# First mixing layer: small products and value products spread over all 24 hops of a round, gate weights in another load, key products later

## What is computed

```python
xr, xw, xk, xv, xa, xg = (h + xx * mu[j] for j in range(6))
r, k, v = xr @ wr, xk @ wk, xv @ wv
a = sigmoid(a0 + (xa @ a1) @ a2)
g = sigmoid(xg @ g1) @ g2
kk = k * k_k normalised per head;  k = k * (1 + (a - 1) * k_a)
# per head of 64: S_t = S_{t-1} diag(w_t) + (S_{t-1} a_t) b_t^T + v_t k_t^T ; y_t = S_t r_t
y = (y - mean) * rsqrt(var + eps) * ln_w + ln_b   # per head
y = (y + sum(r * k * r_k) * v) * g
out = y @ wo
```

## Time and profile before

| | us |
|---|---|
| median of 3 runs | 3449.25 (3448.60 to 3453.86) |
| the profiled execution, device time | 3456.56 |
| its span, first to last instruction | 3454.8 |
| PE / DVE / ACT / POOL busy in the span | 3274.0 / 1647.8 / 754.1 / 362.6 |
| mean granted TensorE clock | 0.974 |

### The profile page before, as it was taken

The page is one execution under the profiler, slowest core; times in us unless marked ns, Lnnn a source line. Parts: engine busy times, 40 slices in busy tenths (PEclk is TensorE's granted clock), DMA queues, the critical chain, the costliest instruction groups (busy, mean ns, idle before and its releaser), DMA issues.

```text
span 3454.8 us, 45620 instructions
## 1 busy us (share of the span) xinstructions
PE 3274.0 (95%) x19462; PEld 2055.7 (60%) x19462; DVE 1647.8 (48%) x3209; ACT 754.1 (22%) x1572; POOL 362.6 (10%) x282
## 2 busy tenths in 40 slices
PE   7999988999999999999999899998999999899998
PEld 3455556888884746788886444544445546434343
DVE  4565675779652226778732666664212304201011
ACT  2333332210013025211002333232223310211111
POOL 0111110222010000132000111113000001000000
PEclk9999998999999999999999999998999999899999
DMA  6322203356641320256522111000211114699997
GB/s 201 122 74 64 69 7 111 110 171 195 194 136 38 98 61 1 61 179 188 170 75 74 49 38 37 26 25 1 70 55 43 49 52 145 284 421 421 421 421 281
DMA packets 355771, 452.46 MB, mean 131 GB/s; under 512 B 25712, under 2 KB 282992, under 8 KB 331760
## 3 DMA queue, kind: packets, MB, share of 16 engines
q1 hardware_dynamic: 355568, 449.55, 38.0%
HBM read 445.27 MB, written 4.20 MB: 130 GB/s over the span
## 4 chain that ended last, share of the span: by engine, by line
PE 83%; DVE 8%; ACT 4%; DMA 3%; issue 1%; SPq 0%; POOLq 0%; POOL 0%; DVEq 0%; ACTq 0%
PE bank L79 82%; DVE A L70 2%; ACT A L87 2%; DMA A<-in_w_up 2%; DVE A L76 1%; DVE A L73 1%; ACT A L86 1%; PE bank L82 1%; DMA W<-in_w_up 1%; DVE A L2023 1%; ACT SM L87 1%; DVE H L70 0%; DVE X L76 0%; DVE X L70 0%; DMA A<-in_x 0%
## 5 line engine op out<-in xcount | busy, mean ns | idle before, releaser
L79 PE MATMUL bank<-A 64*64 64x64 f32 (+6 forms) x8800 | 908.8, 287 | 65.5 <-ACT A L87 37.3
L79 PEld LDWEIGHTS bank<-A 64*64 64x64 f32 (+3 forms) x8800 | 686.1, 157 | 358.3 <-issue 107.7
L79 PE MATMUL bank<-A,W 128*128 128x256 f32 (+1 forms) x2240 | 724.9, 478 | 8.4 <-DMA W<-in_rw_g 7.1
L79 PE MATMUL bank<-H,W 128*128 128x512 f32 (+2 forms) x1712 | 657.2, 528 | 34.1 <-ACT H L87 14.4
L79 PEld LDWEIGHTS bank<-A,W 128*128 128x128 f32 x2240 | 419.9, 191 | 262.4 <-issue 215.3
L87 ACT ACTIVATE A<-bank 128x512 f32<-128x512 f32 (+4 forms) x469 | 194.0, 418 | 1322.0 <-PE bank L79 1225.9
L79 PEld LDWEIGHTS bank<-H,W 128*128 128x128 f32 (+1 forms) x1712 | 309.3, 191 | 275.6 <-issue 238.3
L79 PE MATMUL bank<-A,H 128*64 128x512 f32 (+2 forms) x1224 | 310.7, 574 | 5.4 <-DMA A<-in_w_up 2.6
L70 DVE TENSOR_TENSOR A<-bank,A 128x256 f32<-128x256 f32 (+1 forms) x350 | 157.9, 462 | 195.5 <-PE bank L79 174.7
L87 ACT ACTIVATE A<-A 128x512 f32<-128x512 f32 (+1 forms) x238 | 137.9, 610 | 393.3 <-DVE A L70 362.7
L70 POOL TENSOR_TENSOR A<-A 128x512 f32<-128x512 f32 (+1 forms) x103 | 146.1, 1425 | 709.1 <-PE bank L82 358.7
(11 more groups left out here) (189 smaller groups left out, 2575.4 us busy)
## 6 DMA issues: line engine op xcount, KB each, us to landing
A<-in_w_gate SPq DMA_DIRECT2D x47, 1024.0 KB, 22.7
W<-in_mod_w SPq DMA_DIRECT2D x45, 1024.0 KB, 7.0
A<-in_w_up SPq DMA_DIRECT2D x42, 1024.0 KB, 19.3
A<-in_w_down SPq DMA_DIRECT2D x35, 1024.0 KB, 27.0
W<-in_mlp_up SPq DMA_DIRECT2D x64, 512.0 KB, 5.4
W<-in_mlp_down SPq DMA_DIRECT2D x128, 256.0 KB, 4.0
W<-in_w_mod SPq DMA_DIRECT2D x24, 1024.0 KB, 5.3
W<-in_w_up SPq DMA_DIRECT2D x22, 1024.0 KB, 19.3
```

The costliest lines, as they stand in the source:

```text
L79: return self.e.matmul(o, l, r, start=start, stop=stop, skip_group_check=True)
```

## The change

- PE's fetch products go by a table: four matmuls in hops 2, 5, 8, 11, two in 14, one in 15, three in 17, one each in 22 and 23 (before: four in 14 and four in 17). The v product so ends in hop 23; its ACT copy moves there from hop 18. The small product `row0` of rounds 1 and 2 moves from hop 20 to 17.
- PE's sb halves go to hops 0 and 1 (both in 0 before), sk to 3 and 6 (2 and 4), the variance to 9 (7), bon to 20 (17). The turn of V uses bank 3 instead of 2.
- DVE's masks move with them, and its kh, bh, rkk go to hops 15, 16, 17 (13, 14, 15); the two last post products to hop 16 (14). The transpose of the first mask is now in hop 2, behind the first md step of hop 1.
- POOL's b goes from hop 10 to 14, behind ett; the products "end" to hops 6 and 7 (5 and 6).
- The gate weights of blocks 0 to 3 come with the rv load of blocks 4 to 7, in its free half; the separate rg loads stay for blocks 4 to 7, in rounds 8 to 11.

```diff
+        def gate_parts(ct, off):
+            cs = slice(ct * 128, ct * 128 + 128)
+            return (off, (0, P), (128,), a["rw_g2"][0:128, cs]), (off + 128, (0, 32), (128,), a["rw_g2"][128:160, cs])
...
+        FILL = {2: 4, 5: 4, 8: 4, 11: 4, 14: 2, 15: 1, 17: 3, 22: 1, 23: 1}
+
         def sp_fetch(sp, ct):
             cs = slice(ct * 128, ct * 128 + 128)
             load(sp, ("rk", ct), (0, (0, P), (8, 128), rows128(a["rw_wk"][:, cs])), (1024, (0, P), (8, 128), rows128(a["rw_wr"][:, cs])))
-            load(sp, ("rv", ct), (0, (0, P), (8, 128), rows128(a["rw_wv"][:, cs])))
+            load(sp, ("rv", ct), (0, (0, P), (8, 128), rows128(a["rw_wv"][:, cs])), *(gate_parts(ct - 4, 1024) if ct >= 4 else ()))
...
-            yield from idle(2)
-            for j, name in enumerate(("k", "r", "v")):
-                key = ("rv", ct) if j == 2 else ("rk", ct)
-                s_, there = ring[key]
...
-                b = fbank(ct, j)
-                pe.wait_ge(ring.sems[s_], there)
-                pe.wait_ge(*left[b])
-                for k in range(KT):
+            n = 0
+            for slot in range(24):
+                for n in range(n, n + FILL.get(slot, 0)):
+                    j, k = divmod(n, KT)
+                    name, key = ("k", "r", "v")[j], ("rv", ct) if j == 2 else ("rk", ct)
...
+                    b = fbank(ct, j)
+                    if k == 0:
+                        pe.wait_ge(ring.sems[s_], there)
+                        pe.wait_ge(*left[b])
                     pe.wait_ge(s_dv, ndv["xm", (1, 0, 2)[j], k])
                     m = pe.mm(BK[b][:, :], v[:, k, :], xm[(1, 0, 2)[j]][:, k, :], k == 0, k == 7)
                     if k == 7:
@@ -844,22 +852,21 @@
                             npe.mark_next("free", *key)
                         m.then_inc(s_pe, npe(name, ct))
                         left[b] = (s_ac, nac[name, ct])
...
-                    if k % 4 == 3:
-                        yield from idle(3)
-            if ct in (1, 2):
-                pe_row0(pe, ct - 1)
-            yield from idle(4)
+                n += 1 if slot in FILL else 0
+                if slot == 17 and ct in (1, 2):
+                    pe_row0(pe, ct - 1)
+                yield
...
             for j, (name, dst) in enumerate((("k", Kb2), ("r", Rb2), ("v", V2))):
-                yield from idle(6)
+                yield from idle((6, 6, 11)[j])
...
-            yield from idle(6)
+            yield
...
-            yield from idle(13)
+            yield from idle(16)
             pe.wait_ge(s_dv, ndv["rkk", ct])
             pe.wait_ge(*left[3])
             pe.mm(BK[3][:, :], C("blk"), t0, True, True).then_inc(s_pe, npe("bon", ct))
             left[3] = (s_dv, ndv["bo", ct])
-            yield from idle(7)
...
         def gp_prep(gp, ct):
-            yield from idle(10)
+            yield from idle(14)
             if ct:
                 gp.wait_ge(s_pe, npe["tok", ct - 1, 2])
             gp.wait_ge(s_dv, ndv["kkn", ct])
             gp.wait_ge(s_ac, nac["ab", ct])
             gp.tt(BH, KKb, Ab, MUL).then_inc(s_gp, ngp("b", ct))
-            yield from idle(14)
...
-            yield
+            yield from idle(3)
...
@@ -996,7 +1003,7 @@
             yield
             dv.wait_ge(s_dv, ndv["rh", ct])
             dv.stt(t0, Rb, col("rw_rk", ct), Kb, MUL, MUL).then_inc(s_dv, ndv("rkk", ct))
-            yield from idle(6)
+            yield from idle(4)
...
             score(BH, 4, 0).then_inc(s_pe, npe("sb", ct, 0))
+            yield
             score(BH, 5, 1).then_inc(s_pe, npe("sb", ct, 1))
             yield
...
             pe.wait_ge(*left[2])
             score(KH, 2, 0).then_inc(s_pe, npe("sk", ct, 0))
             left[2] = (s_dv, ndv["sk", ct, 0])
-            yield
-            yield
+            yield from idle(3)
             pe.wait_ge(*left[2])
             score(KH, 2, 1).then_inc(s_pe, npe("sk", ct, 1))
             left[2] = (s_dv, ndv["sk", ct, 1])
-            yield
-            for n, (src, b) in enumerate(((V, 2), (c8(KH), 2), (c8(BH), 3))):
-                yield
-                yield
+            for n, (src, b) in enumerate(((V, 3), (c8(KH), 2), (c8(BH), 3))):
+                yield
+                if n:
+                    yield
                 pe.wait_ge(*((s_gp, ngp["end", ct, n - 1]) if n else (s_ac, nac["v", ct])))
                 pe.wait_ge(*left[b])
                 turn(src, b).then_inc(s_pe, npe("tok", ct, n))
...
-            yield from idle(3)
+            yield from idle(4)
             gp.wait_ge(s_pe, npe["sk", ct, 1])
             gp.wait_ge(s_ac, nac["f", ct])
             for n, src in enumerate((KH, BH)):
                 gp.tt(c8(src), c8(src), per_chunk(Fs[ct % 3]), MUL).then_inc(s_gp, ngp("end", ct, n))
                 yield
-            yield from idle(7)
+            yield from idle(6)
...
-            for n, (dst, b) in enumerate(((Vts[ct % 2], 2), (KHts[ct % 2], 2), (BHts[ct % 2], 3))):
+            for n, (dst, b) in enumerate(((Vts[ct % 2], 3), (KHts[ct % 2], 2), (BHts[ct % 2], 3))):
...
             masked("sb", NRs[ct % 2], 4, 0)
+            yield
             masked("sb", NRs[ct % 2], 5, 1)
             dv.wait_ge(s_dv, ndv.n)
             dv.e.transpose(of16(AM), by16(NRs[ct % 2][:, :, 0, :])).then_inc(s_dv, ndv("raw", ct))
-            yield
...
             for j in range(1, 15):
                 if j not in (1, 8, 12):
                     yield
-                if j == 2:
+                if j == 3:
                     masked("sk", AKs[ct % 2], 2, 0)
-                if j == 4:
+                if j == 6:
                     masked("sk", AKs[ct % 2], 2, 1)
                 solve16(dv, XI, XTMP, j).then_inc(s_dv, ndv() if j < 14 else ndv("inv", ct))
...
         def sp_post(sp, ct):
-            cs = slice(ct * 128, ct * 128 + 128)
-            load(sp, ("rg", ct), (0, (0, P), (128,), a["rw_g2"][0:128, cs]), (128, (0, 32), (128,), a["rw_g2"][128:160, cs]))
+            load(sp, ("rg", ct), *gate_parts(ct, 0))
...
         def pe_post(pe, ct, left):
-            kg, tg = ring["rg", ct]
+            kg, tg = ring["rv", ct + 4] if ct < 4 else ring["rg", ct]
+            off = 1024 if ct < 4 else 0
...
             left[3] = (s_dv, ndv["yc", ct])
-            yield from idle(5)
+            yield from idle(7)
             pe.wait_ge(s_ac, nac["ysq", ct])
             pe.wait_ge(*left[3])
             pe.mm(BK[3][:, :], C("blk"), t2, True, True).then_inc(s_pe, npe("yvar", ct))
             left[3] = (s_dv, ndv["yv", ct])
-            yield from idle(5)
+            yield from idle(3)
             pe.wait_ge(ring.sems[kg], tg)
             pe.wait_ge(s_ac, nac["lo", 4])
             pe.wait_ge(*left[2])
-            pe.mm(BK[2][:, :], wv(kg, 0, (0, P), (128,)), ZG[:, 0:512], True, False)
-            npe.mark_next("free", "rg", ct)
-            pe.mm(BK[2][:, :], wv(kg, 128, (0, 32), (128,)), ZG[0:32, 512:1024], False, True).then_inc(s_pe, npe("g", ct))
+            pe.mm(BK[2][:, :], wv(kg, off, (0, P), (128,)), ZG[:, 0:512], True, False)
+            if ct >= 4:
+                npe.mark_next("free", "rg", ct)
+            pe.mm(BK[2][:, :], wv(kg, off + 128, (0, 32), (128,)), ZG[0:32, 512:1024], False, True).then_inc(s_pe, npe("g", ct))
...
-            yield from idle(6)
+            yield from idle(7)
...
-            yield from idle(12)
+            yield from idle(11)
...
-            yield from idle(5)
...
-            yield from idle(5)
+            yield from idle(6)
             dv.wait_ge(s_pe, npe["yvar", ct])
             dv.ts(t2, BK[3][:, :], 1.0 / 64, 64e-5, MUL, ADD).then_inc(s_dv, ndv("yv", ct))
             yield from idle(3)
...
-            yield from idle(3)
+            yield from idle(4)
             dv.wait_ge(s_ac, nac["yl", ct])
             dv.tt(Yb, Yb, yg[:, ct, :], ADD).then_inc(s_dv, ndv())
             dv.wait_ge(s_dv, ndv.n)
...
             dv.tt(yg[:, ct, :], Yb, BK[2][:, :], MUL).then_inc(s_dv, ndv("post", ct))
-            yield from idle(10)
...
                 if r < 8:
                     sp_fetch(sp, r)
                     sp_mod0(sp, r)
-                if r >= 4:
+                if r >= 8:
                     sp_post(sp, r - 4)
```

More of the change, by code:

```diff
@@ L826, in sp_fetch @@
             load(sp, ("rk", ct), (0, (0, P), (8, 128), rows128(a["rw_wk"][:, cs])), (1024, (0, P), (8, 128), rows128(a["rw_wr"][:, cs])))
-            load(sp, ("rv", ct), (0, (0, P), (8, 128), rows128(a["rw_wv"][:, cs])))
+            load(sp, ("rv", ct), (0, (0, P), (8, 128), rows128(a["rw_wv"][:, cs])), *(gate_parts(ct - 4, 1024) if ct >= 4 else ()))
         def pe_fetch(pe, ct, left):
-            yield from idle(2)
-            for j, name in enumerate(("k", "r", "v")):
-                key = ("rv", ct) if j == 2 else ("rk", ct)
-                s_, there = ring[key]
-                v = wv(s_, 1024 * (j % 2), (0, P), (8, 128))
-                b = fbank(ct, j)
-                pe.wait_ge(ring.sems[s_], there)
```

(14 more changed lines are left out.)

## The result

The changed kernel takes 3470.89 us (median of 6 runs, 3461.49 to 3472.28) where the kernel before takes 3453.58 (6 runs, 3448.60 to 3458.30): a ratio of 1.0046, interval 1.0034 to 1.0058. It is slower by some 16 us, where 27 us less were forecast. The profiled execution took 3471.7 us with a span of 3469.9, against 3456.56 and 3454.8.

What follows compares the result with a forecast made beforehand. PE was taken as the bound, 83% of the chain. Rounds 4 to 7 gave 20.6 us, round 3 1.3, round 8 2, rounds 1, 2 and 9 3: 27 less, 3422 us; range 3408 to 3440 at 0.8.

Steps and rivals of the forecast that it cites:

- the fillings: Work put into hops 1, 3, 6, 9, 15 and 22 hides PE's waits: 6 x 0.49 = 2.9 us a round.
- the solver: Hop 16: with key products moved behind DVE's transposes, PE's wait of 0.95 us at the solver level goes.
- DVE hides it all: Rival: md lands at 6 us or ACT's queue isn't in the way, no 2.0 stall; 41 us gained, 3408; chance 0.13.
- The gate step: Hop 12: gate weights landing with rv remove a wait of 1.78 us and 0.17 of drain, 1.95 us a round.
- One filling of the six: Hop 22: one product matmul put there was to hide 0.49 us a round.
- the md step: Start of round: the later md load makes PE wait in hops 3, 6 and 8; 2.0 us, low 0, high 4.8.
- Two gate issues add 0.8: SP's queue behind rv: two issues of about 0.4 us each, so md lands at 7.6 us into the round.
- The hop by hop working: PE's waits behind md: 0 to 0.2 in hop 3, 0.5 in hop 6, 1.1 for the uu copy; 1.8 to 2.1 together.
- slower: Rival: md lands at 10.1 us or more, rounds 3 to 7 wait 4.8 and PE's clock falls, 2.3 more; 3457; chance 0.07.
- the signs that the prediction named for its failure: DVE waits in hops 16 to 18, mod_w wait past 9 us, clocks under 1.00 in rounds 2 to 7, round 7 above 55.
- Rounds 0, 10, 11: 0, the order of PE's work hardly changes.: First round and last two: no gain or loss counted, 0 us.
- rv is now marked free in hop 23 and not 17: SP's in-order queue: a round's first md load can't be issued before the round begins; named as the edit that costs.

Runs made afterwards that it cites:

- the best kernel: The changed kernel with the ring's turn moved on by four and md loaded ahead of rv on SP: 3417.38 us, ratio 0.9887 to the kernel before.
- the run with the mean later: The changed kernel with the mean four hops later, yc and the squares three: 3463.99 us, ratio 1.0026 to the kernel before.
- the turn: The changed kernel with the ring's turn moved on by four after the rg loads: 3459.32 us, ratio 1.0009 to the kernel before; also added to other runs.
- md first: The changed kernel with SP's order rk, md, md, rv in place of rk, rv, md, md: 3425.31 us, ratio 0.9915 to the kernel before.
- step later: The changed kernel with every md step of DVE one hop later, load as late as there: 3431.01 us, ratio 0.9926 to the kernel before.
- gates alone: The kernel before with only the gate weights of blocks 0 to 3 moved into rv's loads: 3444.02 us, ratio 0.9960.

## Why the prediction was wrong

**Right: what the fillings, the gates and the solver are worth.** 6.0 us a round at the upper clock and 8.3 with a fall were summed; 5.7 and 7.9 to 8.1 were measured once md was out of the way. The rival "DVE hides it all" was priced at 41 us; the best kernel gained 38.5 (3455.92 to 3417.38). The gate step alone was 1.95 and measured 2.0. One filling of the six is not borne out: with hop 22 empty the rounds are as short (50.6), where 0.49 us were summed for it.

**Wrong: the md step, in three places.** It was put at 2.0 us a round (low 0, high 4.8) and took 7.3 to 8.7, with the clock fall in it (58.0 to 59.4 less 50.7). (1) *When it lands.* "Two gate issues add 0.8" gave 7.6 us. SP needed 1.05 to 2.54 us for them, and DVE got md 8.5 to 9.8 us into the round; from rv's issue 8.5 to 9.6, where without gates it was 6.64 and 7.0 and 7.3 in rounds 2 and 3 of the changed kernel. I had counted the parts' issue only, at the least that one takes. The longer issue is not all of it: with the longest, 2.54 us in round 6, md came soonest (8.5 us), and in round 4, with 1.08, latest (9.6). (2) *What stands behind it.* The hop by hop working followed the first state, the second state and lx, and asked for each when PE needs it. It left out yc, on which kn waits for bank 3. That is the 4.26 us. But the run with the mean later shows that the omission was not of one edge: the error was to add small waits on single paths (0.2, 0.5, 1.1). In that run DVE, held up for 5.4 us, works without a gap for 18, and PE's waits come to 5.2. (3) *A solver step at 1.46 us instead of 0.35.* In the kernel before it ran while POOL was idle, but for round 9, where it took 1.35 us beside m (506.10 in DVE's timeline). Now POOL's product m, 1.26 us, starts in the same moment. The rounds of 50.7 us have it too, so it is no large part.

**The stall then drew the clock fall with it.** The rival "slower" had the right mechanism and nearly the right price: 4.8 us of wait and 2.3 of clock a round, 7.1 in all. Measured: 58.0 less 50.7, 7.3, in round 6, 7.5 to 8.7 in the other three. It was given 0.07, for I had it begin at a landing of 9.5 us; the trace shows it at 8.5. The price was luck in part: at a landing of 8.5 us the prediction's path sum gives about 2.9 us (its 2.0 and the 0.9 that md is later), and PE waited 5.1. With 3457 it left out the ring. Of the signs that the prediction named for its failure three are there: a mod_w wait past 9 us in round 4, clocks under 1.00, round 7 above 55 us.

**Missed: round 10.** "Rounds 0, 10, 11: 0, the order of PE's work hardly changes." It was read off PE's work, not the loads. Removing four loads leaves one turn counter at 37 instead of 41, and where the ring goes over to five slots every later load falls on another slot and so on another holder. Some 8 to 12 us of the 3470.89 are this by the medians, 6.3 of them the wait in round 10.

**Also off**: round 8 was to gain 2 us and lost 1.6. It has waits of 3.02 and 2.77 us for DVE, where the longest was 1.78, at a clock of 0.92 as before. Round 3 was to gain 1.3 and lost 1.5, round 2 was to gain 0.5 and lost 3.6, round 9 was to gain 2 and lost 0.4 (34.8 against 34.4).

Together, of the 15.1 us between the profiled spans: 1.7 are there at the first md step (99.00 against 97.31), ahead of the rounds; from there to the end of round 7 (470.1 against 460.6) 7.8 are added, the md step's loss less what the fillings and gates gain; from there to mlp_up's first issue (592.04 against 575.48) 7.1, mostly the turn; and 1.4 are won back behind it, where the code is the same. The value products in hops 22 and 23 (the prediction's "rv is now marked free in hop 23 and not 17") are the edit on which the sign hung: with them in hop 17, and all else as changed, the kernel is 0.8% faster than before instead of 0.5% slower.

What the turn is worth in round 10 is not its wait alone. The turn takes 6.3, 6.9, 6.0 and 4.6 us of PE's wait away (changed kernel, md first, step later, gates alone), and the round gains 6.3, 3.3, 5.9 and 1.1: with md first and with the gates alone the rows ahead of the wait then run at the lower clock, 4.07 us for the gate product instead of 2.18. What isn't settled: why the medians give the turn 8 to 12 us in three of these pairs and 2.5 in the fourth. Behind mlp_up's first issue, where the code is the same, the 13 profiled spans differ by 10 us (2872.6 to 2882.8), without an order that goes with the turn.

## What to carry to other kernels

A load that comes a few us later isn't priced by its own users alone: list what is queued behind the waiting instruction on its in-order engine, and if that engine has no gap soon after, count the whole delay in full, wherever it is collected. Before a load is removed from or added to a ring of slots, redo the slot of every load behind it, above all where the number of slots changes. And a filler that holds a buffer to the end of a round can cost more than the empty slot it fills.

## What the runs showed of the hardware

**The clock can fall behind one short wait.** In the kernel before it fell behind waits of 1.89 and 1.72 us (rounds 5 and 6) and not behind 1.78 (round 7); behind 4.04 to 4.26 it fell each time. In the run with the mean later it did not fall behind 2.27 (the next fetch group took 3.70 us) and fell behind 2.04 (4.09). With no wait over 0.3 us in a round, it stayed at 2.4 GHz in every round of 50.7 us.

**A one-input VectorE step can be held by GpSimd.** The TENSOR_SCALAR of 128x256 takes 0.35 us alone and 1.46 beside POOL's m: it starts at 364.77 and ends at 366.23, 0.16 after POOL's instruction does (364.81 plus 1.26). The prediction took a rule of the Trainium skill (SBUF — State Buffer, SBUF: two separate sides) to mean steps with two inputs only. The page also names VectorE operations in a two-port mode, and this row fits that. It isn't held each time: in round 2 of the changed kernel it starts 0.11 us ahead of POOL's instruction (148.11 and 148.22) and takes 0.35. A transpose is not slowed: in the run with md first one starts at 162.54, wholly beside POOL's product of 1.27 us (162.40), and takes 1.04, as it does alone.

**Small loads ahead of a large one.** Two gate parts of 80 KB together took SP 1.05 to 3.29 us to issue. Where rv goes out at the start of a round, DVE had the first md 6.6 to 7.6 us after rv's issue in rounds without them (once 9.7) and 7.7 to 9.8 in rounds with them. No run takes the parts away and leaves all else, so that they are the cause is argued and not shown.
